# Dense projection tiles placed between the steps of a dilated attention, and weight slots released by a matmul instead of a tile

## The reference, cut to what matters

```python
proj = (n @ w_in[l]).astype(f32)                 # all projections read the same n
rw = proj[..., :RWKV_IN]
rw_prev = jnp.pad(rw, ((0, 0), (1, 0), (0, 0)))[:, :-1]
proj = concatenate([rw + shift_mu * (rw_prev - rw), proj[..., RWKV_IN:]], axis=-1)
(p_r, p_k, p_v, p_wd, p_ad, p_gd, q, k, v, gate_r, gate_a) = split(proj, bounds)
y_rwkv = rwkv7_mix(p_r, p_k, p_v, p_wd, p_ad, p_gd, ...)
y_attn = dilated_mixture(q, k, v)                # 12 heads of 64 in 3 groups of 4
merged = sigmoid(gate_r) * (y_rwkv @ p_rwkv) + sigmoid(gate_a) * (y_attn @ p_attn)
```

## Time and profile before

| What | Value |
|---|---|
| median of three runs | 3747.78 us |
| the profiled execution's own time | 3744.28 us |
| its span, first to last instruction | 3742.5 us |
| mean granted TensorE clock | 0.963 |
| PE busy | 93% of the span |
| DVE / POOL / ACT busy | 46% / 32% / 29% |
| from the sixth `qk` tile's evacuation to the third `rkv0` tile's evacuation | 70.88 to 307.02 us |

### The profile page before, as it was taken

One profiled execution on the slowest core, in us unless ns is written; L12 is line 12 of the kernel. 1 busy time (PEld: TensorE's weight loads), 2 busy tenths in 40 slices (PEclk: granted clock), 3 DMA queues, 4 the chain that ended last, 5 costly groups with the idle time before them and its releaser, 6 DMA issues.

```text
span 3742.5 us, 42937 instructions
## 1 busy us (share of the span) xinstructions
PE 3477.1 (93%) x17184; PEld 2834.3 (76%) x17184; DVE 1732.2 (46%) x2215; ACT 1091.7 (29%) x1651; POOL 1212.2 (32%) x506
## 2 busy tenths in 40 slices
PE   7888889889989889999999999899999999989998
PEld 6666777777868667778788778688878878768886
DVE  1244666666424337776411321567552123137555
ACT  3223233222223332222332222333233222233222
POOL 3202111111134323444233324354433433335443
PEclk9879999999999999999999999999999999999999
DMA  3101010000132216665223222232222322213222
GB/s 129 48 8 46 19 34 32 23 23 28 52 112 97 85 45 213 226 234 209 71 71 105 73 67 85 74 101 90 96 89 68 101 68 82 75 67 105 92 96 74
DMA packets 89094, 319.39 MB, mean 85 GB/s; under 512 B 9792, under 2 KB 11840, under 8 KB 88512
## 3 DMA queue, kind: packets, MB, share of 16 engines
q1 hardware_dynamic: 81360, 297.83, 23.8%
q10 hardware_dynamic: 7536, 18.80, 1.5%
HBM read 312.66 MB, written 3.93 MB: 85 GB/s over the span
## 4 chain that ended last, share of the span: by engine, by line
PE 64%; issue 15%; DVE 11%; POOL 8%; ACT 2%; DMA 1%; POOLq 0%; DVEq 0%; ACTq 0%; SPq 0%
PE bank L541 14%; PE bank L543 14%; PE bank L542 14%; POOL w_lo L491 7%; PE bank L676 5%; PE bank L534 1%; PE bank L536 1%; PE bank L535 1%; PE bank L682 1%; PE bank L1010 1%; PE bank L999 1%; DVE act L1504 1%; DVE arena L1916 1%; PE bank L586 1%; PE bank L651 1%
## 5 line engine op out<-in xcount | busy, mean ns | idle before, releaser
L491 POOL TENSOR_TENSOR w_lo<-w_raw,w_hi 128x1024 fp32r<-128x1024 f32 x468 | 1169.0, 2506 | 1796.6 <-ACT w_hi L1064 1795.0
L541 PE MATMUL bank<-act,w_hi 128*128 128x512 f32 (+1 forms) x3480 | 1398.1, 402 | 67.5 <-DVE act L1504 37.2
L542 PE MATMUL bank<-act,w_hi 128*128 128x512 f32 (+1 forms) x3480 | 1361.8, 391 | 0.0
L543 PE MATMUL bank<-act,w_lo 128*128 128x512 f32 (+1 forms) x3480 | 1361.2, 391 | 0.0
L541 PEld LDWEIGHTS bank<-act,w_hi 128*128 128x128 f32 x3480 | 661.8, 190 | 232.5 <-issue 40.2
L543 PEld LDWEIGHTS bank<-act,w_lo 128*128 128x128 f32 x3480 | 661.5, 190 | 138.4
L542 PEld LDWEIGHTS bank<-act,w_hi 128*128 128x128 f32 x3480 | 663.2, 191 | 128.8 <-issue 4.5
L1064 ACT CAST w_hi<-w_raw 128x1024 fp32r<-128x1024 f32 x468 | 482.4, 1045 | 343.1 <-PE bank L543 187.5
L1071 ACT ACTIVATE arena<-bank 128x512 f32<-128x512 f32 (+1 forms) x227 | 125.4, 557 | 597.9 <-PE bank L543 502.9
L503 POOL TENSOR_TENSOR stats<-stats,exponent 128x8 f32<-128x8 f32 (+2 forms) x33 | 43.6, 1322 | 717.9 <-DVE stats L1525 580.3
L676 PEld LDWEIGHTS bank<-arena 128*128 128x128 f32 x1920 | 234.2, 197 | 53.8 <-DVE arena L1781 19.3
(11 more groups left out here) (235 smaller groups left out, 3126.5 us busy)
## 6 DMA issues: line engine op xcount, KB each, us to landing
w_raw<-in_weights SPq DMA_DIRECT2D x468, 512.0 KB, 3.5
arena<-in_ada SPq DMA_DIRECT2D x96, 512.0 KB, 3.8
arena<-in_strips ACTq DMA_DIRECT2D x8, 448.0 KB, 3.3
arena<-in_x ACTq DMA_DIRECT2D x4, 512.0 KB, 11.6
arena<-in_x ACTq DMA_DIRECT2D x1, 2048.0 KB, 8.9
out_y<-arena SPq DMA_DIRECT2D x1, 2048.0 KB, 6.3
y_scratch<-tmp ACTq DMA_DIRECT2D x7, 256.0 KB, 2.4
arena<-y_scratch ACTq DMA_DIRECT2D x1, 1792.0 KB, 8.6
```

Of the source, the lines that this page charges most:

```text
L491: nc.gpsimd.tensor_tensor(w_lo[:, k, :], w_raw[:, k, :], w_hi[:, k, :].bitcast(F32), ALU.subtract).then_inc(sem("w_low"), 1)
L541: nc.tensor.matmul(o, wh, xh, start=first, stop=False)
L542: nc.tensor.matmul(o, wh, xl, start=False, stop=False)
L543: mm = nc.tensor.matmul(o, wl, xh, start=False, stop=last)
```

## The change

1. **Two halves.** The weights of q, k and v are reordered (`w_in_attn`) so that the stages are `qk0` (six tiles: q and k for heads hh 0 and 1 of each group), `v0` (384 columns as 4 units, 4 token tiles), `qk1` and `v1`. The attention starts after `qk0` and `v0`.
2. **Dense blocks between the steps.** The 16 tiles of `qk1`, `v1`, `lora` and `rkv0` (128 blocks) are run inside the attention by `slot(it, part)`: part 0 stands between `scores(it)` and `turn(it-1)`, part 1 between `turn(it-1)` and `weigh(it-1)`. The list is ten blocks after the first scores, then 5 + 5 per step for seven steps, then 3 + 3 per step for eight.
3. **One bank for them.** These 16 tiles all use bank 3 (`beside_attention`); the first block of each waits for the evacuation of the one before it. All other tiles go round the banks as before, by a table (`place`).
4. **ACT and DVE in the attention.** ACT evacuates these tiles and casts weight units at the same places (`take_slot`), in front of `turned_out(it-1)` for part 0 and behind the exponential for part 1. DVE shifts the finished `lora` and `rkv0` tiles between `weights(it-1)` and the scores of `it` (`shift_slot`).
5. **Buffers.** RAW, LORA, GD, R, K, V no longer share memory with the attention's. RAW is cleared in front of the attention; KX0, BX0, VX0, AX0 are cleared behind it, with `low(q_attn + 1)` later than before; the copies of V wait for that (`rw_expanded`).
6. **Slots released by their last matmul**, in the whole kernel: where the last block of a unit is not the last of its tile, that matmul signals `unit_used`, and the cast and the low half of unit u+4 wait for it instead of the whole tile.
7. **`follow` on token-major tiles:** as long as the next tile uses the same units, it casts up to the tile's own last unit and no further; the two units beyond are cast only in front of the evacuation of the last token tile.
8. Behind the attention PE goes straight to the first tile of `rkv1`, then waits for `lora_ready`. The plan has two units more (v was 6, is 8).

```diff
+    def beside_attention(self, first, last):
+        for t in range(self.stages[first][0], self.stages[last][1]):
+            self.tiles[t]["bank"] = BANKS - 1
...
-    p.plain("qk", "w_in", 0, 3360, 12)
-    p.token_major("v", "w_in", 0, 3360 + 1536, 768, TC)
+    for half in range(2):
+        p.plain(f"qk{half}", "w_in_attn", 0, 768 * half, 6)
+        p.token_major(f"v{half}", "w_in_attn", 0, 1536 + 384 * half, 384, TC)
...
+    UNIT_FREE, within = {}, 0
+    for u in sorted(last_block):
+        t, i = last_block[u]
+        if i == len(tiles[t]["blocks"]) - 1:
+            UNIT_FREE[u] = ("tile_done", t + 1)
+        else:
+            within += 1
+            UNIT_FREE[u] = ("unit_used", within)
...
+        NOW = list(range(stages["qk1"][0], stages["v1"][1])), list(range(stages["lora"][0], stages["rkv0"][1]))
+        SLOTS = [(0, 10)] + [(5, 5)] * 7 + [(3, 3)] * 8
...
             for it in range(4 * TC + 1):
                 if it < 4 * TC:
                     scores(it)
+                    slot(it, 0)
+                if it == 1:
+                    all_evacuated(pe, "v0")
                 if it >= 1:
                     turn(it - 1)
+                if it < 4 * TC:
+                    slot(it, 1)
+                if it >= 1:
                     weigh(it - 1)
-            stage("lora", "n_mix")
-            pe.wait_ge(sem("lora_ready"), 3)
+            pe.wait_ge(sem("att_scored"), 4 * TC)
...
             def follow(t):
-                last = min(max(u for u, _, _ in tiles[t]["blocks"]) + 2, n_units - 1)
+                T = tiles[t]
+                again = T["rows"] and tiles[t + 1]["blocks"][0][0] == T["blocks"][0][0]
+                last = min(max(u for u, _, _ in T["blocks"]) + (0 if again else 2), n_units - 1)
...
-                        act.wait_ge(sem("tile_done"), last_tile[u - RING] + 1)
+                        unit_free(act, u - RING)
...
+            def take_slot(it, part):
+                for t in slot_tiles(it, part):
+                    if t < stages["lora"][0]:
+                        take_operand(t)
+                    else:
+                        to_raw(t, t - stages["lora"][0])
+                if slot_pieces(it, part):
+                    cast_to(slot_units(it, part))
...
             for it in range(4 * TC):
                 c = it % TC
+                take_slot(it, 0)
                 if it >= 1:
                     turned_out(it - 1)
                 act.wait_ge(sem("att_max"), it + 1)
...
+                take_slot(it, 1)
```

More of the change, by code:

```diff
@@ L116, in token_major, with place @@
         self.stages[name] = (start, len(self.tiles))
+    def beside_attention(self, first, last):
+        for t in range(self.stages[first][0], self.stages[last][1]):
+            self.tiles[t]["bank"] = BANKS - 1
+    def place(self):
+        on, uses, nxt = {}, [0] * BANKS, 0
+        for t, T in enumerate(self.tiles):
+            b = T.setdefault("bank", nxt)
+            nxt = (b + 1) % BANKS
+            uses[b] += 1
+            T["use"], T["previous"] = uses[b], on.get(b)
+            on[b] = t
+            T["on"] = dict(on)
     def split(self, name, buf, n, free_after):
@@ L176, in make_plan @@
         p.unit("none")
+    p.place()
     return p
@@ L251, in build_program @@
         base = free_at[0]
[L253 to L259, removed]
         free_at[0] = 0
@@ L608, in _, with slot @@
             spread(banks[4])
-            stage("qk", "n_mix")
-            stage("v", "n_mix")
-            all_evacuated(pe, "v")
+            stage("qk0", "n_mix")
+            stage("v0", "n_mix")
+            def slot(it, part):
+                for n in slot_pieces(it, part):
+                    tile((NOW[0] + NOW[1])[n // KT], splits["n_mix"][0], only=n % KT)
             def scores(it):
@@ L717, in side @@
                 mm.then_inc(sem("side_made"), 1)
-            t0 = stages["rkv0"][0]
+            t0 = stages["rkv1"][0]
             n_mix = splits["n_mix"][0]
-            for t in range(t0, t0 + 4):
-                tile(t, n_mix)
+            tile(t0, n_mix)
+            pe.wait_ge(sem("lora_ready"), 3)
             side("zw", 0)
             side("za", 0)
-            tile(t0 + 4, n_mix)
+            tile(t0 + 1, n_mix)
             side("ks", 0)
             side("kb", 0)
-            tile(t0 + 5, n_mix)
+            tile(t0 + 2, n_mix)
             side("bo", 0)
@@ L883, in _ @@
                     x_queries(hd + 1)
-                    t = stages["x_q"][0] + 2 * hd + 4
-                    for before in range(t - BANKS, t):
-                        evacuated(pe, before)
+                    for t in tiles[stages["x_q"][0] + 2 * hd + 3]["on"].values():
+                        evacuated(pe, t)
                 pe.wait_ge(sem("x_p"), hd + 1)
@@ L1185, in spread_a @@
                 done(ins, "rw_ax")
-            for i in range(3):
-                raw(0, i)
             half_tanh("zw", 0, SW, 0)
             half_tanh("za", 0, A_, 8)
-            follow(stages["rkv1"][0])
+            high(q_attn + 1)
             key_squares(0)
@@ L1639, in side_emptied @@
                 do(ins, "side_emptied", SIDE_AT[name, p] + 1)
-            def shifts(p, which):
-                for i in which:
-                    shift(stages[f"rkv{p}"][0] + i, 3 + 3 * p + i, 8 * i + p, (R, K, V)[i])
             def keys(p):
@@ L1714, in finish @@
                 do(V_.memset(spare, 0.0), "y_out" if p + 1 < PAIRS else "tmp_ready")
-            shifts(0, (0, 1, 2))
-            keys(0)
             decay_sums(0)
+            for a in (VX0, AX0):
+                do(V_.memset(a, 0.0))
+            do(V_.memset(spare, 0.0), "rw_expanded")
+            low(q_attn + 1)
             key_statistic(0)
@@ L2168, in lay_out @@
     names["w_in_pair"] = w_in[:, :, order]
+    group = [np.arange(P) + P * (2 * g + half) for half in range(2) for g in range(3)]
+    q, v = np.concatenate(group), np.concatenate(group) + 1536
+    order = np.concatenate([q[0:384], q[0:384] + 768, q[384:], q[384:] + 768, v])
+    names["w_in_attn"] = w_in[:, :, 3360 + order]
     f = np.float32
```

162 lines of the change are left out of this document (106 added, 56 removed).

## The result

The changed kernel takes 3690.12 us (median of four runs, 3687.96 to 3693.16), the kernel before 3746.59 (four runs, 3743.23 to 3750.36). The ratio is 0.985 with a 95% interval of 0.9833 to 0.9867: 56.5 us less. The time is inside the predicted range of 3684 to 3727, 11 us under the predicted 3701 and 1 under the likeliest case's own range of 3691 to 3712.

A forecast was written before the change was run, and what follows sets the result against it. PE, 93% busy, was taken to bound the kernel, recoverable only in gaps and low clock. Terms -38.4 (attention stretch), -14 (`mem_v`) and +5.4 (`ret_v`) sum to -47.0, giving 3701 us, range 3684 to 3727.

The forecast's parts named there:

- the likeliest case: Whole kernel: the main forecast of 3701 us, chance 0.58, with its own range of 3691 to 3712.
- low clock: Attention with dense blocks inside: mean granted clock 0.94, a cost of 10 us; 0.97 would cost 5, 0.75 about 50.
- The prediction's marker: Rebuilt attention stretch: evacuation of the third `rkv0` tile about 38 us earlier, near 269 us.
- hand-overs, and ACT late at them: Bank 3 in the attention: twelve hand-overs of 0.86 us, 10.3, plus 5.0 for ACT's lateness at tile ends.
- `v0`: Ahead of the attention: four tiles of 4.16 us, 16.6, plus 3.4 for late third and fourth units; sum 20.0.
- The RWKV pairs: Prelude of the pairs, 29.9 us behind the attention: change of 0, at most 3 us either way.
- `mem_v`: `mem_v` with first `x_q` tile: slots released early cut 46.7 us to 32.7, gain 14, between 6 and 17.
- `ret_v`: Retention heads: `follow` without its two units delays the first `ret_g` unit, loss 5.4 us, between 0 and 10.
- The clock stays low: Rival, attention: dense blocks don't lift the clock above 0.75, 40 us more, 3741 us; chance 0.10.
- The chain of `n_x`: Rival, `mem_v`: this chain takes over and casts bind, so early release gives 2 us at most, 3713; chance 0.12.
- Slower than before by ACT's order: Rival, attention: exponentials queue behind ACT's evacuations or casts; decides from 2.9 us a step, 3765 at 4; chance 0.04.
- DVE and POOL: Rival, attention: 16 low halves on POOL each delay DVE's shifts by 1.7 us, 27 us lost, 3728; chance 0.10.

The follow-up runs named there:

- the idle matmuls: Kernel before plus four unused 128 x 512 matmuls in front of each `turn` and each `weigh`, 128 in all; 0.9966 of the kernel before.
- the 48 blocks: Changed kernel with `qk1` and `v1` ahead of the attention, only `lora` and `rkv0` blocks inside, three a step; 0.9864 of the kernel before.
- the run with two units ahead: Changed kernel with `follow` casting two units ahead again where a token-major stage has at most two units (`ret_v`); 0.9836 of the kernel before.
- parts 6 and 7 alone: Kernel before with only slots released by their last matmul and `follow` without its two units; 0.9966 of the kernel before, 13 us less.
- the aligned slots: Changed kernel with 4 + 4 blocks a step, so each inserted tile ends at a slot's end; 0.9805 of the kernel before.

## Why the prediction came out right, and where its terms were off

The sign, the mechanism and the range held. Behind the 11 us between 3701 and 3690 are mainly three things: the cost of the low clock was put too high, the pairs lost time that no term held (which worked the other way), and the profiled executions lie off their medians, the one under and the other over. By the prediction's steps:

**The attention.** The prediction's marker was set wrong: it looked for the third `rkv0` evacuation near 269 us, but in the new order that comes at 253.5, ahead of the last value products. The same piece of work ends in both kernels where the first matmul of `rkv1` starts: 306.82 before, 260.17 after, 46.6 us apart, where the terms give 38.4. From the first scores (91.58) it is 168.6 us; the terms without `v0` give 177.7:

| Term | Predicted | Measured |
|---|---|---|
| the attention's own matmuls | 69 | 69.8 (L695 27.6, L724 27.8, L709 14.4) |
| 16 dense tiles | 81.9 | 81.9, taken over, not measured apart |
| hand-overs, and ACT late at them | 10.3 + 5.0 | 13.8 (11.7 idle, and 12 x 0.17) |
| last `weigh` | 1.5 | 1.4 |
| low clock | 10 | 1.7 |
| sum | 177.7 | 168.6 |

The 0.17 is what an idle time in the records leaves out: a matmul is shown for 0.40 us while the next could start after 0.23. The term that was mis-sized is the low clock, "I take 0.94 on the mean, a cost of 10". It was 0.99, better than both bounds of 0.97 and 0.75, with one drop of 3.4 us. That it is the blocks that hold the clock is shown by the idle matmuls (0.98) and the 48 blocks (1.00), and that few gaps are not needed for it by the run with all blocks in part 0 (0.98 with 31.1 us idle). Why it is better than in the mix behind 337 us is open. The prediction's reading of the earlier trace rows was also too narrow: in the 34 us at 1.2 GHz PE ran not only scores and value products but 17 of the attention's transposes too, and the same mix had run at 0.99 in the 21 us before.

`v0` was put at 20.0 and took 20.8: less idle time than the 3.4 us (1.94 and 0.28), but the clock in it was 0.92, some 1.7 us. That is the best of seven traces; with the same code it took up to 2.2 us more.

**The RWKV pairs** were put at 0 and lost 3.1 us to the clock, with the same instructions. This is the scatter of such a stretch: between the same two statistics (126.9 us before) the run with two units ahead, whose code up to there is that of the changed kernel, lost 1.1 us, and the other runs lie between 1.2 us lost and 1.7 won. The changed kernel's trace has the largest loss of them all.

**`mem_v`** was put at 14, measured 13.8 (57.3 less 43.4), and 13.7 with parts 6 and 7 alone, so it doesn't hang on the rest of the change. The prediction gave it all to the release; that ACT no longer casts ahead of the first token tile's evacuation changed there too, and no run separates the two. **`ret_v`**, the term that spoke against the change, was put at +5.4, measured +5.9, and went away with the two units.

**The sum.** 46.6 - 3.2 + 13.8 - 0.2 - 5.9 = 51.1 in the traces, against 47.0. The attention stretch gave 8.2 more than forecast and the pairs took 3.2 of that back, so it is partly luck that the sum comes so near. The rest of the 11 us is the choice of executions: before's profile was put 3.5 under its median, and after's lies 3.0 over its own.

**The rivals.** *The clock stays low* is refuted: 0.99. *The chain of `n_x`*: refuted by 13.8 us at `mem_v`. *Slower than before by ACT's order*: every hand-over in mid-slot is that mechanism in small, and with all tile ends in part 1 it costs 18.6 us, 1.2 a step, far from the 2.9 that decide; with all blocks in part 0 ACT's casts stood in front of a copy once for a wait of 4.45 us. *DVE and POOL*: in the changed kernel the shift is slowed (its second operation takes 2.72 us beside POOL's low half, and 0.75 without), and PE waits for it not once. The rival counted sixteen such meetings, the trace has three: two of the shifts' operations and one scaling. With POOL's work doubled 2.2 us reach PE, and by another road than the rival named. The Trainium skill (SBUF — State Buffer, "Who interferes with whom") says that a VectorE operation with two SBUF inputs blocks against a GpSimd one that reads SBUF; the trace agrees, with the 2.72 us against 0.75. What it costs is a question of the slack behind.

Of the 46.6 us, I work out from the earlier trace rows that the gaps of the attention gave about 26 (117.1 less 69 of own work less 22 for the clock), the low clock 22, and its neighbours `v`, `lora` and `rkv0` some 20; the hand-overs, the stalls of `v0` and the drop took back about 20 of the sum. This split is an estimate, no experiment makes all of it.

## What to carry to other kernels

Work that is put into the gaps of a chain of small matmuls pays twice, for the gap and for the clock; read the granted clock of the stretch before you count gaps. Put the ends of the inserted tiles where PE turns to its other work anyway: here this was worth another 17 us for changing one line of numbers, while 48 blocks had done as much as 128 without it. Release a ring slot by the last instruction that reads it, but look at each stage for whether its look-ahead should shrink with that: for two units in four slots it should not (5 us), and for four units it was done here, without a run that kept it.

## What the hardware showed that I had not expected

- 128 useless matmuls, 29 us of work, made the kernel 13 us faster (0.9966), and the granted clock of the attention rose from 0.75 to 0.98.
- The same attention instructions on PE took 117.1 us at 0.75 in one kernel and 122.6 at 0.70 in another, where it started 4.8 us sooner and two low halves of POOL lay at its start: the 4.8 us won ahead of it were lost in it, and 0.8 more.
- In the changed kernel PE's clock fell inside the attention only once, right behind an idle time of 1.87 us, but not behind one of 1.88 us 38 us later. With all blocks in part 1 it fell behind 3.08 us and not behind 3.32. With no wait over 1.4 us (the aligned slots) it did not fall at all. So the length of one idle time doesn't tell whether it falls.
